# Two reorderings ahead of the expert stage: tiles of normalised tokens turned as 1, 2, 0, and the expert gate broadcast before the rank products

## The reference, cut to what matters

```python
x = x + g1 * _merge_branches(o_na, o_swa, o_ret, ga, gs, gre, p)
h2 = _rms(x, p["norm2_g"]) * (1 + sc2) + sh2
x = x + g2 * _hier_moe(h2, p)
...
# in _hier_moe
g_logit = (x @ p["router_group_w"] + p["router_group_b"])
...
e_logit = (x @ p["router_expert_w"] + p["router_expert_b"])
...
e_top, e_sel = lax.top_k(e_in, TOP_K_EXPERT)
w = jax.nn.softmax(e_top, axis=-1) * p_group
...
a = jax.nn.silu(hg) * hu * combine.astype(x.dtype)[..., None]
y = jnp.einsum('nef,efd->nd', a, p["w_down"])
```

## Time and profile before

| | us |
|---|---|
| median of three runs | 1250.97 |
| the profiled execution's own time | 1252.71 |
| its span in the profile | 1250.4 |
| TensorE busy | 1124.9 (90%) |
| VectorE busy | 684.7 (55%) |
| ScalarE busy | 430.6 (34%) |
| GpSimd busy | 176.0 (14%) |

### The profile page before, as it was taken

The page is one execution under the profiler, slowest core; times in us unless marked ns, Lnnn a source line. Parts: engine busy times, 40 slices in busy tenths (PEclk is TensorE's granted clock), DMA queues, the critical chain, the costliest instruction groups (busy, mean ns, idle before and its releaser), DMA issues.

```text
span 1250.4 us, 19119 instructions
## 1 busy us (share of the span) xinstructions
PE 1124.9 (90%) x7645; PEld 952.1 (76%) x7645; DVE 684.7 (55%) x1445; ACT 430.6 (34%) x927; POOL 176.0 (14%) x228
## 2 busy tenths in 40 slices
PE   3889999999899899999849999999999989999970
PEld 1667778897787689999737677888999768999960
DVE  1434565545376656666663336655447665666663
ACT  2432345622323423333232233554233342322221
POOL 0011140000020121111031113100002112111103
PEclk9999999999999999999969999999999999999995
DMA  9798882247736459999557899122643644999934
GB/s 318 237 246 220 235 279 69 68 140 258 247 135 235 152 170 344 374 377 371 169 169 208 223 223 275 52 68 73 195 155 104 254 151 166 342 373 376 377 103 169
DMA packets 135178, 272.01 MB, mean 218 GB/s; under 512 B 7152, under 2 KB 89232, under 8 KB 126896
## 3 DMA queue, kind: packets, MB, share of 16 engines
q1 hardware_dynamic: 118992, 219.13, 50.8%
q0 software_dynamic: 15488, 50.01, 14.3%
q10 hardware_dynamic: 608, 1.62, 0.4%
HBM read 248.71 MB, written 22.02 MB: 217 GB/s over the span
## 4 chain that ended last, share of the span: by engine, by line
PE 78%; DVE 8%; DMA 7%; ACT 2%; issue 2%; POOL 2%; SPq 0%; DVEq 0%; ACTq 0%; POOLq 0%
PE ps L1114 18%; PE ps L775 15%; PE ps L904 14%; PE ps L1154 6%; PE ps L1036 5%; PE ps L1051 4%; DMA ring<-in_w_in 4%; PE ps L664 3%; DMA ring<-in_ada_w 2%; PE ps L1106 2%; PE ps L848 2%; PE ps L888 1%; PE ps L870 1%; DMA arena<-scratch_ys,slot_i 1%; PE ps L1161 1%
## 5 line engine op out<-in xcount | busy, mean ns | idle before, releaser
L556 DVE TENSOR_TENSOR w_lo<-ring,w_hi 128x512 fp32r<-128x512 f32 x128 | 87.9, 691 | 154.4 <-ACT w_hi L545 154.4
L545 ACT ACTIVATE w_hi<-ring 128x512 fp32r<-128x512 f32 x128 | 80.4, 631 | 226.5 <-PE ps L775 149.7
L553 DVE TENSOR_TENSOR w_lo<-ring,w_hi 128x512 fp32r<-128x512 f32 x128 | 89.2, 698 | 117.2 <-ACT w_hi L543 117.2
L904 PE MATMUL ps<-h_hi,w_hi 128*128 128x384 f32 x384 | 134.2, 350 | 7.7 <-ACT arena L2118 4.7
L543 ACT ACTIVATE w_hi<-ring 128x512 fp32r<-128x512 f32 x128 | 79.9, 628 | 165.0 <-PE ps L904 100.4
L775 PE MATMUL ps<-w_hi,h_hi 128*128 128x512 f32 x288 | 117.5, 408 | 13.6 <-DVE h_lo L1349 7.6
L904 PE MATMUL ps<-h_hi,w_lo 128*128 128x384 f32 x384 | 128.8, 335 | 0.0
L904 PE MATMUL ps<-h_lo,w_hi 128*128 128x384 f32 x384 | 128.7, 335 | 0.0
L775 PE MATMUL ps<-w_lo,h_hi 128*128 128x512 f32 x288 | 114.4, 397 | 0.0
L775 PE MATMUL ps<-w_hi,h_lo 128*128 128x512 f32 x288 | 113.9, 396 | 0.0
L1114 PEld LDWEIGHTS ps<-arena,ring 128*128 128x128 f32 x960 | 109.7, 192 | 1.6
(11 more groups left out here) (309 smaller groups left out, 2189.3 us busy)
## 6 DMA issues: line engine op xcount, KB each, us to landing
ring<-in_ada_w SPq DMA_DIRECT2D x48, 1024.0 KB, 9.9
ring<-in_w_in SPq DMA_DIRECT2D x48, 1024.0 KB, 5.5
ring<-in_w_down SPq DMA_DIRECT2D x18, 1024.0 KB, 9.1
ring<-in_w_up SPq DMA_DIRECT2D x16, 1024.0 KB, 7.8
ring<-in_w_gate SPq DMA_DIRECT2D x14, 1024.0 KB, 8.3
scratch_ys<-arena POOLq DMA_DIRECT2D x30, 384.0 KB, 6.6
arena<-in_w_gate SPq DMA_DIRECT2D x10, 1024.0 KB, 7.4
ring<-in_w_out SPq DMA_DIRECT2D x8, 1024.0 KB, 4.9
```

What stands on the lines that cost most here:

```text
L545: eng.activation(w_hi[:, q % 2], ring[:, slot, 2 * q:2 * q + 2, :], ACT.Copy).then_inc(whi_ready, 1)
L553: eng.tensor_tensor(gate_weights(w_lo, q), ring[:, SLOT[seg, l, c], k0:k0 + 4, j * P:(j + 1) * P], gate_weights(w_hi, q).bitcast(F32), ALU ...
L556: eng.tensor_tensor(w_lo[:, q % 2], ring[:, SLOT[seg, l, c], 2 * q:2 * q + 2, :], w_hi[:, q % 2].bitcast(F32), ALU.subtract).then_inc(wlo_ ...
L904: mm = pe.matmul(ps[:, bank, 0:TOK], gate_weights(wx, q)[:, kk, :], hx[:, k, :], start=(k == 0 and n == 0), stop=(k == KT - 1 and n == 2))
```

## The change

The three tiles are turned in the order 1, 2, 0, on TensorE and in ScalarE's copies; the router's small sums still follow the first tile turned, which now is tile 1. The gate's broadcast goes ahead of the rank products, and waits only for two copies, those of tiles 1 and 2, whose banks 2 to 5 it overwrites. The `keep_clock` that stood behind it stays behind the rank products and the wait for all three copies, and has five products in place of three.

```diff
-                for t in range(TILES):
+                for t in (1, 2, 0):
                     for k in range(KT):
                         mm = pe.transpose(ps[:, 2 * t + k // 4, (k % 4) * P:(k % 4 + 1) * P], hT[:, k, t * P:(t + 1) * P], ident)
                     mm.then_inc(h2_psum, 1)
-                    if t == 0:
+                    if t == 1:
                         pe.wait_ge(loT_ready, l + 1)
...
+                pe.wait_ge(h2_ready, l * TILES + 2)
+                broadcast_moe_gate(l)
                 ones = cst[:, C_ONE:C_ONE + 1].to_broadcast([P, P])
                 pe.wait_ge(hot_ready, l * 2 + 1)
                 pe.matmul(ps[:, 6, 64:128], cst[:, C_BEFORE:C_BEFORE + P], hotsum[:, 0:4, :].rearrange("p t e -> p (t e)"),
...
                 pe.wait_ge(h2_ready, l * TILES + TILES)
-                broadcast_moe_gate(l)
-                keep_clock(7, 3)
+                keep_clock(7, 5)
                 pe.wait_ge(places_ready, l * 2 + 2)
...
-                for t in range(TILES):
-                    act.wait_ge(h2_psum, l * TILES + t + 1)
+                for n, t in enumerate((1, 2, 0)):
+                    act.wait_ge(h2_psum, l * TILES + n + 1)
                     act.activation(xn[:, t, :].rearrange("p (k h q) -> p k h q", k=KT, h=2),
```

## The result

Over 22 runs of each (three of those of the kernel before are the ones shown ahead), the changed kernel has a median of 1257.94 us and the kernel before 1252.62 us. The ratio is 1.0035, 95% interval 1.002 to 1.0049: **slower by 0.35%**, some 4.4 us (the two medians by themselves lie 5.32 us apart). I had forecast 1250.3 against 1250.97, a ratio of 0.9995, with 0.86 on a difference within 0.2%, and a range that ended at 1252.4. The three runs shown before lay at the low end of what this kernel does: runs of both kernels spread over some 10 us, and the mean granted clock goes with it (in a later group, 0.973 in a run of the kernel before of 1250.75 us, 0.963 in one of 1259.83 us). So the ratio is what counts.

A forecast was written before the change was run, and what follows sets the result against it. TensorE's queue was taken as the path, VectorE's chain only about half a microsecond behind. Gains of 0.39 us and, in layer 1, 0.27, together 0.66, take 1250.97 to 1250.3 us; range 1248.8 to 1252.4.

The forecast's parts named there:

- What bounds, and the size of the gain: TensorE's queue up to the gather is the path, VectorE's selection next; gather 0.39 us earlier in layer 0, 0.27 in layer 1.
- the slip of 0.08 to 0.09 that I charged for the ranks: Rank products queued behind the moved broadcast end later, so VectorE's chain slips 0.08 us in layer 0, 0.09 in layer 1.
- Broadcast at 2.4 GHz behind the transposes: The gate's broadcast, moved behind the transposes, runs at full clock: eight records in 3.4 us, against 6.8 at 1.2 GHz.
- The second rival: Broadcast at half clock: ranks 3.5 us late, VectorE waits, 1257.1 us in all; chance 0.03.
- `keep_clock` of five: Ten records on TensorE after the rank products end at 438.4, ahead of the places; the four added cost nothing.
- the fall: Clock falls in TensorE's new idle time before the places' product: 1252.0 us in one layer, 1253.7 in both; chance 0.12.
- a sign of being wrong: Among the signs named for the changed profile: a granted clock of 0.50 over L1161, the gathering product.
- that rival: Clock falls in the new idle time before the places' product, low over L1097 and L1161: 1.7 us a layer; chance 0.12.
- Low stretch elsewhere gone: Layer 1's first products, at 0.50 from 650.36 to 655.10, lose their low stretch: 2.4 us less, 1247.9 us; chance 0.07.
- the sum: Earlier start of the gathering product L1161 in both layers, 0.39 and 0.27 us, together 0.66 us gained.

The follow-up runs named there:

- The kernel before without filler: The kernel before with keep_clock(7, 3) taken out behind the broadcast, nothing else changed: 1.0007 of before, interval 0.9987 to 1.0028; second profiled execution 1256.35 us.
- the broadcast-alone kernel: The changed kernel with tiles in the old order 0, 1, 2, the early broadcast waiting for all three copies: 1.0026 of before, interval 1.0002 to 1.005.

## Why the prediction was wrong

- *What bounds, and the size of the gain:* right in the main. VectorE's chain takes over as forecast; the gather starts 0.50 and 0.39 us earlier where 0.39 and 0.27 stood. Most of the difference is the slip of 0.08 to 0.09 that I charged for the ranks: VectorE's first use of them did not move. The source of the gain was seen too narrowly: I put TensorE's lateness down to the half clock under the broadcast, and leaving out the three products of `keep_clock` brought the same 0.50 with the half clock still there; filling the idle time ahead of the broadcast brought 0.48 with the three products still there. Either was enough.
- *Broadcast at 2.4 GHz behind the transposes:* right. The clock is 1.00 over 430.40 to 434.10, eight records in 3.70 us. The rule of the Trainium skill that I weighed against it ("TensorE: Matmul & The Clock Gate", Part 4: PE-mode transpose) is not borne out here: the clock stays at 1.00 over the transposes, which have 22 products of the router among them, and over the broadcast behind them. Whether transposes can raise a low clock no run here shows. The second rival did not happen.
- *`keep_clock` of five "cost nothing: VectorE's chain covers them, with 1.6 us of idle time left":* **this is the step that failed.** The records did cost nothing and the idle time came out at 1.75 us, near the 1.6. What failed is that I put the idle time itself at nothing: I took it for harmless, on one row of 1.67 us that was followed by 1.00, and gave the fall 0.12. It happened in four passes of six, and the granted clock over the gather that I had named as a sign of being wrong was there. One case was too few to go by: the row with 2.23 us that was followed by 0.50 stood beside it (and was itself followed by 1.00 in another profile), and where the outcome differs from pass to pass, a single row at a nearby length says little.
- *The price in that rival, 1.7 us a layer:* too small. I took the low stretch under the broadcast, 3.38 us long. In the first profile the clock was low for 6.9 us from the places' product on, and over the four passes the gather lost 2.9 us on average. With 2 × 4/6 of it the sum becomes +3.0 us, between the two measured results.
- *In the kernel before* the same loss of clock was paid under the broadcast, where VectorE's chain hid all but at most some 0.5 us of it, and TensorE then worked without a pause into the gather. The change repaired the clock where it cost little and let it fall where each microsecond counts.
- *Low stretch elsewhere gone:* layer 1's first products have the low clock from 653.32 to 656.02 in the first profile of the change, 2.7 us against 4.74, but over 4.74 us again in the second. The kernel before without filler has them both ways too, so the change cannot be credited with it.

The absolute number was also bound to three runs at the low end of the spread. That is a matter of the median, not of the ratio.

The forecast gain itself is not confirmed as a time. With six or seven products the change stands at 0.9996, 0.9991 and 1.0005 of before: level, with the 0.9995 of the forecast inside each interval. No version here beats the kernel before clearly. With six or seven products the change showed no fall in six passes, so either is a better form of it than five.

## What to carry to other kernels

When an idle stretch of TensorE is moved, look at what follows it in its new place: idle time under cover is harmless only if the work behind it is under cover too. Filler that keeps the clock up should reach to about where the critical work starts; by the 0.43 us of a record, a product too many costs up to 2 × 0.43 us; a gap of 1.75 us cost 2.9 in four passes of six. Judge such a gap from several profiles, since one pass may show nothing.

## What the runs showed of the hardware that was not expected

After an idle time of only 1.31 us the gather took 8.72 us at a granted clock of 0.62 on average, and after 1.75 us the clock fell or held in two passes of one execution. What decides the single pass is open. Behind such a gap the low clock lasted 6.9 us over the gather's products of 96 columns, against 3.38 us over the broadcast's of 512; in the broadcast-alone kernel it was shorter, with a gather of 7.22 us at 0.76, so by the same working (1 − 0.76) × 2 × 7.22 = 3.5 us. The width of the products alone therefore does not decide how long it lasts; what does stays open.
